# Who subtracts the first 192 columns of a weight slab

## The chip, the cores and the metric

The kernel runs on one core of a Trainium2 chip. The metric is the device time in microseconds (us) of one execution. The engines are TensorE (PE, its weight loads PEld), VectorE (DVE), ScalarE (ACT), GpSimd (POOL) and SyncE (SP), which here only starts DMAs. Each runs its own list of instructions in order, and they meet at semaphores.

## The reference

A sequence of 256 tokens of width 1024 goes through two stacks of two layers each. All products have fp32 weights. Cut to what matters:

```
for i in range(2):                                  # first stack
    proj = rmsnorm(x) @ w_in[i]                     # q, k, v, conv, ssm input, gates
    x = x + (gates * (attention, short conv, s5 scan)) @ w_mix_o[i]
    gt, up = split(rmsnorm(x) @ w_ffn_in[i])
    x = x + (silu(gt) * up) @ w_ffn_out[i]
x = rmsnorm(x)
for l in range(2):                                  # second stack
    u = rmsnorm(x) @ w_in_2[l]                      # retention, ssd, dt, gates
    x = x + (gates * (retention, ssd)) @ w_o_2[l]
    x = x + (silu(gate) * up) @ w_down_2[l]         # as above, other weights
return rmsnorm(x)
```

## The kernel before

All weights are one stream of 696 slabs of 128 x 1024 fp32 in DRAM, read in order (136 slabs for each layer of the first stack, 212 for each of the second). A slab is eight blocks of 128 x 128. To keep the precision, each slab is split in two fp32r halves: `w_hi` is the slab cast to fp32r, `w_lo` is `w_raw - w_hi`. Activations are split in the same way, and each product is three matmuls (L550 hi*hi, L551 hi*lo, L552 lo*hi; in slabs whose result is wanted by rows, L620 to L622), so an ordinary slab costs PE 24 matmuls of 256 columns.

A slab passes through a ring of four slots (`RING`), and the work on it is ordered by semaphores:

- SP loads slab s into `w_raw[s % 4]` when `w_lo` of slab s-4 is done.
- ACT casts it to `w_hi` (L1011) when it has landed and PE has finished slab s-4, and bumps `hi_done`. In ACT's list this cast stands three slabs ahead (`AHEAD`), between its other work.
- POOL subtracts columns 192 to 1023 (L509, `lo_g`). It has nothing else to do after its start: it goes from slab to slab as fast as `hi_done` comes.
- DVE subtracts columns 0 to 191 (L1316, `lo_v`), by a call `split(at, i + AHEAD)` that is written into its list of work at the head of each slab's other work. Whatever stands before it in DVE's list comes first.
- PE starts a slab when both `lo_v` and `lo_g` have come (L539) and the PSUM bank is free.

The order of PE, ACT and DVE is written out by hand in `tasks1`, `tasks2` and `ffn`. Three places are spoken of below.

**The first half of the feed-forward part** (44 slabs, in each of the four layers; a loop over pairs of slabs, gate and up, 88 pairs in all). For each pair b, DVE scales the gate bank (L1366, `f_act`), ACT applies SiLU to it (L1051), DVE multiplies it by the up bank (L1370), scales the product (L1372), casts it to `f_hi` (L1376) and subtracts for `f_lo` (L1378). DVE has a `split` behind L1366 and one behind L1372. ACT casts one slab before the SiLU of a pair and one behind it:

```
split(now, si + 2 * b + 1 + AHEAD)
act.wait_ge(v_gate, now.ffn + (b + 1))
nc.scalar.activation(f_act[:, b, :], f_act[:, b, :], ACT.Silu).then_inc(out[(ti + 2 * b) % 4], 1)
split(now, si + 2 * b + 2 + AHEAD)
```

The SiLU frees the gate's bank, in which PE puts the gate of pair b + 2.

**The value slabs of the second stack** (16 slabs in 8 pairs in each layer, L620 to L622). DVE has nothing to evacuate here; it computes the softplus for `dt`, a chain of some twenty dependent operations on 128 x 64 elements (L1745 to L1770), and stands its splits behind it.

**The gate slabs and the ssd output slabs of the second stack**, where DVE's list holds the roots (L1794 to L1798), the turned `xdt` (L1806), `cbm` (L1814) and the normed `s_hi`, `s_lo` (L1844 to L1849), and PE waits for them.

Of the kernel before, what the change touches and what calls it, by code (L numbers as in the profile page):

```python
# [20 lines left out]
ALU = mybir.AluOpType  # L21
# [13 lines left out]
RING = 4  # L35
AHEAD = 3
LO_V = 192
FF = 22
# [171 lines left out]
def hybrid_kernel(nc, weights, x_t, p1_d, p2_d, c1_d, c2_d, decay_d, out_t):  # L210
    with ExitStack() as ctx:
# [137 lines left out]
        hi_done = sem("hi_done")  # L349
        lo_v = sem("lo_v")  # L350
        lo_g = sem("lo_g")
# [129 lines left out]
        def _(sp):  # L481
# [6 lines left out]
            with sp.Fori(1, TOTAL // RING + 1) as it:  # L488
                for slot in range(RING):

                    sp.wait_ge(lo_v, it * RING + (slot + 1 - RING))
                    sp.wait_ge(lo_g, it * RING + (slot + 1 - RING))
                    load(it * RING + slot, slot)
# [9 lines left out]
        @block.gpsimd  # L503
        def _(pool):
            nc.gpsimd.memset(zpad[:, 0:8], 0.0).then_inc(pad_ok, 1)
            with pool.Fori(0, TOTAL // RING) as it:
                for slot in range(RING):
                    pool.wait_ge(hi_done, it * RING + (slot + 1))
                    nc.gpsimd.tensor_tensor(w_lo[:, slot, LO_V:], w_raw[:, slot, LO_V:],  # L509
                                            w_hi[:, slot, LO_V:].bitcast(F32), ALU.subtract).then_inc(lo_g, 1)  # L510
            for slot in range(AHEAD):
                pool.wait_ge(hi_done, TOTAL + slot + 1)
                nc.gpsimd.tensor_tensor(w_lo[:, slot, LO_V:], w_raw[:, slot, LO_V:],
                                        w_hi[:, slot, LO_V:].bitcast(F32), ALU.subtract).then_inc(lo_g, 1)


        @block.tensor
        def _(pe):
# [13 lines left out]
            def weights_of(at, i):  # L532

                pe.wait_ge(lo_v, at.slab + (i + 1))
                pe.wait_ge(lo_g, at.slab + (i + 1))
# [759 lines left out]
        def _(dve):  # L1295
# [15 lines left out]

            def split(at, i):

                slot = i % RING
                dve.wait_ge(hi_done, at.slab + (i + 1))
                tt(w_lo[:, slot, 0:LO_V], w_raw[:, slot, 0:LO_V], w_hi[:, slot, 0:LO_V].bitcast(F32), SUB).then_inc(lo_v, 1)  # L1316

            def gained(at, second, b):
# [34 lines left out]
            def ffn(at, second):  # L1353
                si, ti, so, to = ffn_layout(second)
                gained(at, second, KD - 1)
                split(at, si + AHEAD)
                root_of(at, 1)
                with dve.Fori(0, FF // 2) as it:
                    now = Later(at, it, 4, 4, 2)
                    for b in range(2):  # L1360
# [5 lines left out]
                        tt(f_act[:, b, :], acc[(t - 1) % 4][:, 0:T], rinv[:, :], MUL).then_inc(v_gate, 1)  # L1366
                        split(now, gate_slab + 1 + AHEAD)
                        wait_used(dve, now, gate_slab + 1)
# [3 lines left out]
                        tt(f_prod[:, b, :], f_prod[:, b, :], rinv[:, :], MUL).then_inc(v_prod, 1)  # L1372
                        split(now, gate_slab + 2 + AHEAD)
                        dve.wait_ge(v_prod, now.ffn + (b + 1))
# [4 lines left out]
                for n in range(KD):  # L1379
                    for m in range(3):  # L1380
                        if n or m:
                            split(at, so + 3 * n + m + AHEAD)
                    wait_used(dve, at, so + 3 * n + 2)
# [211 lines left out]
            def first_slab(at, own, i):  # L1595
                split(at, i + AHEAD)
                bank = acc[i % 4]
# [63 lines left out]
            dve.wait_ge(consts, 32)  # L1661
            start = Layer(False, 0)
            for slot in range(AHEAD):
                split(start, slot)
            dve.wait_ge(pad_ok, 1)
# [465 lines left out]
```

## Time and profile before

| | us |
|---|---|
| median of 3 runs | 2668.67 (2667.32 to 2669.65) |
| span of the profiled execution | 2667.1 |
| PE busy | 2381.9 (89%) |
| DVE busy | 1792.1 (67%) |
| POOL busy | 1486.3 (56%) |
| ACT busy | 1240.4 (47%) |
| DMA read | 373.5 MB, 140 GB/s over the span |

The profiled execution's time is its span, 2667.1 us, 1.6 us below the median. A busy share is an average over stages with different limits, so it doesn't say which engine sets the time; for that one asks in each stage which wait ends last. A row of the timeline gives the start, the duration, and in brackets how long the engine stood idle before it and for whom. "Busy" contains the time that an instruction spends blocked after its start.

### The profile page before, as it was taken

The page shows a single profiled execution, that of the slowest core. Times are in us where ns is not written, and L with a number is a line of the kernel's source. Part 1 is how long each engine was busy: PE and PEld are TensorE (multiplying, and loading weights), DVE is VectorE, ACT ScalarE, POOL GpSimd, SP SyncE. Part 2 cuts the span into 40 slices and gives each one's busy share as a digit, 9 for nine tenths or more (in the row PEclk, how much of TensorE's full clock was granted, in tenths as well). Part 3 has the DMA queues.
Part 4 walks back from the last instruction along what each step waited for, and adds up shares of the span by engine and source line. Part 5 has one row for each costly group of instructions (what it writes and reads, how often), then busy time and mean ns, then how long its engine had stood idle before and what let it go on. Part 6 is the DMA issues. An engine that isn't in the chain of part 4 may idle for free.

```text
span 2667.1 us, 53618 instructions
## 1 busy us (share of the span) xinstructions
PE 2381.9 (89%) x18844; PEld 2281.2 (86%) x18844; DVE 1792.1 (67%) x2602; ACT 1240.4 (47%) x1744; POOL 1486.3 (56%) x704
## 2 busy tenths in 40 slices
PE   5798699987787899988989998999889989979998
PEld 5788699887787899888989888999889889879988
DVE  5876769738976499284784467696465773485992
ACT  4243355542243555443543662654435536645554
POOL 4344466664444466755546455667565555456666
PEclk9899899988888899989999999999899999999999
DMA  4233344543233354544434334445544344334444
GB/s 162 91 108 103 103 150 164 175 160 103 88 111 111 111 167 168 193 143 144 141 113 165 127 111 158 155 164 178 167 147 160 122 140 146 119 127 166 165 161 171
DMA packets 104265, 377.19 MB, mean 141 GB/s; under 512 B 11408, under 2 KB 13712, under 8 KB 103824
## 3 DMA queue, kind: packets, MB, share of 16 engines
q1 hardware_dynamic: 101888, 368.10, 40.5%
q10 hardware_dynamic: 2192, 6.52, 0.7%
q8 instruction: 129, 2.11, 0.3%
q14 instruction: 56, 0.46, 0.1%
HBM read 373.52 MB, written 1.05 MB: 140 GB/s over the span
## 4 chain that ended last, share of the span: by engine, by line
PE 57%; DVE 26%; issue 11%; ACT 5%; DVEq 1%; DMA 1%; ACTq 0%
PE acc L550 15%; PE acc L551 14%; PE acc L552 14%; DVE f_hi L1376 6%; ACT w_hi L1011 2%; PE mid L673 2%; DVE zs L1509 1%; PE mid L524 1%; DVE w_lo L1316 1%; DVE f_act L1366 1%; PE acc L620 1%; PE acc L621 1%; PE acc L622 1%; DVE r_hi L1868 1%; PE mid L901 1%
## 5 line engine op out<-in xcount | busy, mean ns | idle before, releaser
L509 POOL TENSOR_TENSOR w_lo<-w_raw,w_hi 128x832 fp32r<-128x832 f32 x696 | 1479.6, 2132 | 1168.1 <-ACT w_hi L1011 1166.5
L1011 ACT CAST w_hi<-w_raw 128x1024 fp32r<-128x1024 f32 x699 | 726.6, 1047 | 401.1 <-PE acc L552 384.0
L550 PE MATMUL acc<-h_hi,w_hi 128*128 128x256 f32 x2240 | 665.8, 297 | 55.9 <-DVE w_lo L1316 45.9
L1316 DVE TENSOR_TENSOR w_lo<-w_raw,w_hi 128x192 fp32r<-128x192 f32 x699 | 394.4, 569 | 453.7 <-ACT w_hi L1011 434.0
L551 PE MATMUL acc<-h_lo,w_hi 128*128 128x256 f32 x2240 | 647.1, 289 | 0.0
L552 PE MATMUL acc<-h_hi,w_lo 128*128 128x256 f32 x2240 | 645.7, 288 | 0.0
L550 PEld LDWEIGHTS acc<-h_hi,w_hi 128*128 128x128 f32 x2240 | 444.1, 198 | 66.6 <-DVE w_lo L1316 48.3
L551 PEld LDWEIGHTS acc<-h_lo,w_hi 128*128 128x128 f32 x2240 | 444.2, 198 | 0.8
L552 PEld LDWEIGHTS acc<-h_hi,w_lo 128*128 128x128 f32 x2240 | 443.0, 198 | 0.0
L550 PE MATMUL acc<-g_hi,w_hi 128*128 128x256 f32 x1376 | 397.1, 289 | 10.1 <-ACT f_act L1051 0.5
L552 PE MATMUL acc<-g_hi,w_lo 128*128 128x256 f32 x1376 | 386.4, 281 | 0.0
L551 PE MATMUL acc<-g_lo,w_hi 128*128 128x256 f32 x1376 | 386.3, 281 | 0.0
L550 PEld LDWEIGHTS acc<-g_hi,w_hi 128*128 128x128 f32 x1376 | 259.4, 189 | 33.4 <-issue 23.2
L551 PEld LDWEIGHTS acc<-g_lo,w_hi 128*128 128x128 f32 x1376 | 259.6, 189 | 0.0
L552 PEld LDWEIGHTS acc<-g_hi,w_lo 128*128 128x128 f32 x1376 | 259.4, 188 | 0.0
L550 PE MATMUL acc<-f_hi,w_hi 128*128 128x256 f32 x704 | 205.8, 292 | 15.3 <-DVE f_lo L1378 13.7
L552 PE MATMUL acc<-f_hi,w_lo 128*128 128x256 f32 x704 | 200.0, 284 | 0.0
L551 PE MATMUL acc<-f_lo,w_hi 128*128 128x256 f32 x704 | 199.9, 284 | 0.0
L1378 DVE TENSOR_TENSOR f_lo<-f_prod,f_hi 128x256 f32 x88 | 183.6, 2086 | 10.8
L1376 DVE CAST f_hi<-f_prod 128x256 f32 x88 | 181.0, 2057 | 0.0
L550 PEld LDWEIGHTS acc<-f_hi,w_hi 128*128 128x128 f32 x704 | 135.5, 192 | 18.3 <-DVE f_lo L1378 14.5
L1051 ACT ACTIVATE f_act<-f_act 128x256 f32<-128x256 f32 x88 | 36.9, 420 | 229.1 <-DVE f_act L1366 229.0
(347 smaller groups left out, 4317.1 us busy)
## 6 DMA issues: line engine op xcount, KB each, us to landing
w_raw<-weights_d SPq DMA_DIRECT2D x700, 512.0 KB, 3.3
p<-p_d ACTq DMA_DIRECT2D x2, 1080.0 KB, 5.4
rdec<-decay_d ACTq DMA_DIRECT2D x2, 768.0 KB, 5.7
x<-x_d ACTq DMA_DIRECT2D x1, 1024.0 KB, 11.3
out_d<-work SPq DMA_DIRECT2D x4, 256.0 KB, 2.2
c<-c_d ACTq DMA_DIRECT2D x1, 712.0 KB, 12.4
p<-p_d ACTq DMA_DIRECT2D x2, 244.0 KB, 2.8
c<-c_d ACTq DMA_DIRECT2D x1, 448.0 KB, 4.0
```

The lines of the kernel that those rows point to most:

```text
L509: nc.gpsimd.tensor_tensor(w_lo[:, slot, LO_V:], w_raw[:, slot, LO_V:], w_hi[:, slot, LO_V:].bitcast(F32), ALU.subtract).then_inc(lo_g, 1)
L524: part = mm(mid[0][:, 0:T], con1("ones_d"), work[:, b, :], start=b == 0, stop=b == KD - 1)
L550: mm(dst, wh, hi[:, k, :], start=first and j == 0, stop=False)
L551: mm(dst, wh, lo[:, k, :], start=False, stop=False)
L552: done = mm(dst, wl, hi[:, k, :], start=False, stop=last and j == len(ks) - 1)
L620: mm(dst, hh, wh, start=k == 0, stop=False)
L673: last = mm(dst, b, u[rows, blk, c * CH:(c + 1) * CH], start=True, stop=True, tile_position=(PC * q, 0))
L1011: nc.scalar.copy(w_hi[:, slot, :], w_raw[:, slot, :]).then_inc(hi_done, 1)
L1051: nc.scalar.activation(f_act[:, b, :], f_act[:, b, :], ACT.Silu).then_inc(out[(ti + 2 * b) % 4], 1)
L1316: tt(w_lo[:, slot, 0:LO_V], w_raw[:, slot, 0:LO_V], w_hi[:, slot, 0:LO_V].bitcast(F32), SUB).then_inc(lo_v, 1)
L1376: copy(f_hi[:, k, :], f_prod[:, b:b + 1, :]).then_inc(ff_hi, 1)
L1378: tt(f_lo[:, k, :], f_prod[:, b:b + 1, :], f_hi[:, k, :].bitcast(F32), SUB).then_inc(ff_lo, 1)
```

## The change

The constant `LO_V` and DVE's `split` go. POOL subtracts all 1024 columns of each slab. The semaphore `lo_v` goes, and with it SP's wait and PE's wait for it. Nothing else is moved.

```diff
-LO_V = 192
...
-                    sp.wait_ge(lo_v, it * RING + (slot + 1 - RING))
                     sp.wait_ge(lo_g, it * RING + (slot + 1 - RING))
                     load(it * RING + slot, slot)
...
-                    nc.gpsimd.tensor_tensor(w_lo[:, slot, LO_V:], w_raw[:, slot, LO_V:],
-                                            w_hi[:, slot, LO_V:].bitcast(F32), ALU.subtract).then_inc(lo_g, 1)
+                    nc.gpsimd.tensor_tensor(w_lo[:, slot, :], w_raw[:, slot, :],
+                                            w_hi[:, slot, :].bitcast(F32), ALU.subtract).then_inc(lo_g, 1)
...
-                pe.wait_ge(lo_v, at.slab + (i + 1))
                 pe.wait_ge(lo_g, at.slab + (i + 1))
...
-            def split(at, i):
-
-                slot = i % RING
-                dve.wait_ge(hi_done, at.slab + (i + 1))
-                tt(w_lo[:, slot, 0:LO_V], w_raw[:, slot, 0:LO_V], w_hi[:, slot, 0:LO_V].bitcast(F32), SUB).then_inc(lo_v, 1)
...
                         tt(f_act[:, b, :], acc[(t - 1) % 4][:, 0:T], rinv[:, :], MUL).then_inc(v_gate, 1)
-                        split(now, gate_slab + 1 + AHEAD)
...
                         tt(f_prod[:, b, :], f_prod[:, b, :], rinv[:, :], MUL).then_inc(v_prod, 1)
-                        split(now, gate_slab + 2 + AHEAD)
                         dve.wait_ge(v_prod, now.ffn + (b + 1))
...
             def second_slab(at, own, i):
-                split(at, i + AHEAD)
```

The other calls of `split` in DVE's list (in `first_slab`, in the second half of the feed-forward part and three at the start) go in the same way.

DVE's list in the first half of the feed-forward part, one pair, before; the names in brackets are the semaphores waited for:

```order
L1366 TENSOR_TENSOR f_act<-acc,rinv 128x256 [waits out3,used]
L1316 TENSOR_TENSOR w_lo<-w_raw,w_hi 128x192 [waits hi_done]
L455 REGISTER_ALU
L1370 TENSOR_TENSOR f_prod<-f_act,acc 128x256 [waits out2,used]
L1372 TENSOR_TENSOR f_prod<-f_prod,rinv 128x256 [waits out3]
L1316 TENSOR_TENSOR w_lo<-w_raw,w_hi 128x192 [waits hi_done]
L1374 REGISTER_ALU
L1376 ISA [waits v_prod]
L1376 COPY f_hi<-f_prod 128x256
L1378 REGISTER_ALU [waits ff_hi]
L1378 TENSOR_TENSOR f_lo<-f_prod,f_hi 128x256
```

The same pair now (the lines have moved up by 11 to 13):

```order
L1355 TENSOR_TENSOR f_act<-acc,rinv 128x256 [waits out3,used]
L453 REGISTER_ALU
L1358 TENSOR_TENSOR f_prod<-f_act,acc 128x256 [waits out2,used]
L1360 TENSOR_TENSOR f_prod<-f_prod,rinv 128x256 [waits out3]
L1361 REGISTER_ALU
L1363 ISA [waits v_prod]
L1363 COPY f_hi<-f_prod 128x256
L1365 REGISTER_ALU [waits ff_hi]
L1365 TENSOR_TENSOR f_lo<-f_prod,f_hi 128x256
```

The two subtractions are gone and the cast to `f_hi` stands directly behind the second product.

DVE's list at the value slabs, the end of the `dt` chain, before:

```order
L1768 SCALAR_TENSOR_TENSOR dts<-dts 128x64 [waits dve_step2]
L1769 REGISTER_ALU
L1770 SCALAR_TENSOR_TENSOR dts<-dts 128x64 [waits dve_step2]
L1315 REGISTER_ALU
L1316 TENSOR_TENSOR w_lo<-w_raw,w_hi 128x192 [waits hi_done]
L1315 REGISTER_ALU
L1316 TENSOR_TENSOR w_lo<-w_raw,w_hi 128x192 [waits hi_done]
```

And now:

```order
L1748 SCALAR_TENSOR_TENSOR dts<-dts 128x64 [waits dve_step2]
L1749 REGISTER_ALU
L1750 SCALAR_TENSOR_TENSOR dts<-dts 128x64 [waits dve_step2]
L1712 ISA
L1715 SCALAR_TENSOR_TENSOR cv<-acc,p_130,cv 128x255 [waits a_cv]
```

Nothing that PE needs for its value slabs stands behind the chain any more; the next thing in the list is the convolution of the slabs that follow.

## Rows read from the trace of the kernel before

**Rows 1.** The page: the chain that ended last, shares of the span by engine.
```profile
PE 57%; DVE 26%; issue 11%; ACT 5%; DVEq 1%; DMA 1%; ACTq 0%
```

**Rows 2.** Waits of PE on VectorE's share: us in total, times, longest us.
```profile
PE acc L550 <- DVE w_lo L1316: 57.4, 14, 8.0
PE acc L620 <- DVE w_lo L1316: 13.4, 2, 6.7
```

**Rows 3.** Groups and single lines: durations in ns, minimum/median/maximum or mean.
```profile
L1316 DVE TENSOR_TENSOR w_lo<-w_raw,w_hi 128x192 fp32r<-128x192 f32 x699 | 394.4, 569 | 453.7 <-ACT w_hi L1011 434.0
...
L509 POOL TENSOR_TENSOR w_lo<-w_raw,w_hi x696: 1926/2146/4034, 5.5 to 2646.4; 128x832 fp32r<-128x832 f32 x174
L505 POOL MEMSET zpad<- x1: 105/105/105, 0.7 to 0.7; 128x8 f32 x1
L1376 DVE CAST f_hi<-f_prod x88: 2021/2048/2093, 373.6 to 2592.2; 128x256 f32 x88
L1378 DVE TENSOR_TENSOR f_lo<-f_prod,f_hi x88: 1980/2004/2200, 375.7 to 2594.4; 128x256 f32 x88
```

**Rows 4.** Timeline of VectorE, feed-forward, second layer: start us, duration us, what.
```profile
956.55 0.41 DVE L1366 TENSOR_TENSOR f_act<-acc,rinv 128x256 f32<-128x256 f32 x1
...
957.45 0.42 DVE L1370 TENSOR_TENSOR f_prod<-f_act,acc 128x256 f32<-128x256 f32 x1 [0.22 <-ACT f_act L1051]
957.90 0.42 DVE L1372 TENSOR_TENSOR f_prod<-f_prod,rinv 128x256 f32<-128x256 f32 x1
958.39 0.36 DVE L1316 TENSOR_TENSOR w_lo<-w_raw,w_hi 128x192 fp32r<-128x192 f32 x1
958.71 2.03 DVE L1376 CAST f_hi<-f_prod 128x256 f32 x1
960.86 2.00 DVE L1378 TENSOR_TENSOR f_lo<-f_prod,f_hi 128x256 f32 x1
962.78 0.41 DVE L1366 TENSOR_TENSOR f_act<-acc,rinv 128x256 f32<-128x256 f32 x1
...
967.10 2.20 DVE L1378 TENSOR_TENSOR f_lo<-f_prod,f_hi 128x256 f32 x1
969.23 0.41 DVE L1366 TENSOR_TENSOR f_act<-acc,rinv 128x256 f32<-128x256 f32 x1
```

**Rows 5.** Timelines of GpSimd and ScalarE in the same stretch.
```profile
958.43 4.15 POOL L509 TENSOR_TENSOR w_lo<-w_raw,w_hi 128x832 fp32r<-128x832 f32 x2 [2.08 <-ACT w_hi L1011]
964.67 2.17 POOL L509 TENSOR_TENSOR w_lo<-w_raw,w_hi 128x832 fp32r<-128x832 f32 x1 [2.09 <-ACT w_hi L1011]
967.03 1.99 POOL L509 TENSOR_TENSOR w_lo<-w_raw,w_hi 128x832 fp32r<-128x832 f32 x1 [0.20 <-ACT w_hi L1011]
...
957.00 0.42 ACT L1051 ACTIVATE f_act<-f_act 128x256 f32<-128x256 f32 x1 [1.41 <-DVE f_act L1366]
957.32 1.99 ACT L1011 CAST w_hi<-w_raw 128x1024 fp32r<-128x1024 f32 x2
```

**Rows 6.** Timeline of PE there: first matmul of a gate slab, of an up slab.
```profile
957.47 0.39 PE L550 MATMUL acc<-g_hi,w_hi 128*128 128x256 f32 x1
...
960.69 0.36 PE L550 MATMUL acc<-g_hi,w_hi 128*128 128x256 f32 x1
```

**Rows 7.** Value slabs: stretches with busy us (x matmuls first) and PEclk; PE's wait.
```profile
1237.10:1242.70 5.60, 5.57 (x26) 5.58 (x27) 0.51 (x2) 0.00 (x0) 0.00 (x0) 0.51 0.75 257
1997.10:2002.70 5.60, 5.54 (x34) 5.55 (x35) 0.54 (x3) 0.00 (x0) 0.00 (x0) 0.71 0.75 257
1245.30:1251.10 5.80, 5.80 (x50) 5.77 (x49) 1.56 (x2) 2.54 (x4) 4.14 (x2) 1.00 0.14 34
...
1237.13 0.58 PE L620 MATMUL acc<-w_hi,h_hi 128*128 128x256 f32 x1 [6.72 <-DVE w_lo L1316]
```

**Rows 8.** Gate and ssd slabs: the same columns (us, PE, PEld, DVE, ACT, POOL).
```profile
1354.70:1402.40 47.70, 34.68 (x267) 33.16 (x265) 46.43 (x74) 17.21 (x26) 25.79 (x12) 0.90 0.33 111
1588.20:1621.20 33.00, 19.47 (x130) 18.45 (x128) 32.10 (x40) 9.70 (x13) 15.70 (x7) 0.90 0.18 64
```

More of the change, by code:

```diff
@@ L349, in hybrid_kernel @@
         hi_done = sem("hi_done")
-        lo_v = sem("lo_v")
         lo_g = sem("lo_g")
@@ L508, in _ @@
                     pool.wait_ge(hi_done, it * RING + (slot + 1))
-                    nc.gpsimd.tensor_tensor(w_lo[:, slot, LO_V:], w_raw[:, slot, LO_V:],
-                                            w_hi[:, slot, LO_V:].bitcast(F32), ALU.subtract).then_inc(lo_g, 1)
+                    nc.gpsimd.tensor_tensor(w_lo[:, slot, :], w_raw[:, slot, :],
+                                            w_hi[:, slot, :].bitcast(F32), ALU.subtract).then_inc(lo_g, 1)
             for slot in range(AHEAD):
                 pool.wait_ge(hi_done, TOTAL + slot + 1)
-                nc.gpsimd.tensor_tensor(w_lo[:, slot, LO_V:], w_raw[:, slot, LO_V:],
-                                        w_hi[:, slot, LO_V:].bitcast(F32), ALU.subtract).then_inc(lo_g, 1)
+                nc.gpsimd.tensor_tensor(w_lo[:, slot, :], w_raw[:, slot, :],
+                                        w_hi[:, slot, :].bitcast(F32), ALU.subtract).then_inc(lo_g, 1)
         @block.tensor
@@ L1355, in ffn @@
                 gained(at, second, KD - 1)
-                split(at, si + AHEAD)
                 root_of(at, 1)
@@ L1379, in ffn @@
                 for n in range(KD):
-                    for m in range(3):
-                        if n or m:
-                            split(at, so + 3 * n + m + AHEAD)
                     wait_used(dve, at, so + 3 * n + 2)
@@ L1661, in _ @@
             dve.wait_ge(consts, 32)
-            start = Layer(False, 0)
-            for slot in range(AHEAD):
-                split(start, slot)
             dve.wait_ge(pad_ok, 1)
@@ L1851, in second_slab @@
             def second_slab(at, own, i):
-                split(at, i + AHEAD)
                 bank = acc[i % 4]
```

## Prediction, made before the changed kernel ran

> **What bounds the kernel now.** I read the chain that ended last, then PE's waits, then each stage's timeline. The chain runs 57% over PE and 26% over VectorE, and not at all over GpSimd by name [rows 1]. That is where care is needed: a VectorE instruction that is blocked by GpSimd counts as VectorE's.
>
> The chip shows the block plainly in the first half of the feed-forward part. VectorE's cast to f_hi and its subtraction for f_lo take 2.0 to 2.2 us in all 88 pairs [rows 3], while a product of the same 256 columns takes 0.42 [rows 4]. The cast starts at 958.71, 0.28 us after a GpSimd subtraction that started at 958.43, and ends at 960.74; the two GpSimd instructions there take 4.15 together, so the first ends near 960.5. The f_lo subtraction starts at 960.86 and ends at 962.86, behind the second one (958.43 + 4.15 = 962.58) [rows 4, 5]. On the other side, VectorE's share of w_lo at 958.39 starts 0.04 before GpSimd and takes 0.36, undisturbed [rows 4, 5]. At 967.10 an f_lo subtraction that starts 0.07 after GpSimd is blocked for 2.20. The rule that I read from this: of two such instructions the one that starts first keeps the other out until it ends; products with an operand in PSUM (f_act, the first f_prod) are free. The Trainium skill, SBUF — State Buffer, section "SBUF: two separate sides", calls it an exclusive lock on a port pair that GpSimd shares with VectorE, taken by VectorE's two-input operations and its two-port modes; by that rule, the trace agrees.
>
> So a pair of slabs there is a closed loop: f_act starts, SiLU on ScalarE, ScalarE's casts of w_hi, two GpSimd subtractions, the end of f_lo, next f_act. It takes 962.78 - 956.55 = 6.23 us in one parity and 969.23 - 962.78 = 6.45 in the other, 6.34 on average. PE is a passenger: it starts a gate slab at 957.47, 0.05 after SiLU has freed the bank, and an up slab at 960.69, just after GpSimd's w_lo [rows 5, 6]. PE needs 48 matmuls for the pair, at the full clock 50 of them in 5.8 us [rows 7], so 5.6 us: it has 0.7 us to spare in each.
>
> Elsewhere PE waits directly for VectorE's share of w_lo, 57.4 + 13.4 = 71 us in 16 places [rows 2]. There the subtraction itself is short; it stands behind other VectorE work.
>
> **The GpSimd instruction.** Undisturbed, 832 columns take 1.93 us, the minimum [rows 3]; the median 2.15 has about 0.2 us of waiting for VectorE's share, which starts just before. 8 columns of a memset take 0.105 [rows 3]. So (1.93 - 0.10) / 832 = 2.2 ns per column, and 192 more cost 0.42 us: 2.35. In proportion to the median it would be 2.15 x 1024 / 832 = 2.64, 0.49 more; against that median an instruction that no longer waits would be only 0.2 longer. I take 0.42 where GpSimd starts freely now, 0.2 where it waits for VectorE's share, and keep 0.2 to 0.49 as bounds. The Trainium skill, GPSIMD Engine Reference, section 3.1, gives 4497 ns for a tensor_tensor of 2048 fp32 columns, so by estimate 2.25 us for 1024, against 2293 ns on VectorE, and its rule for elementwise work is to use VectorE. By that price the sum below would be 0.1 us smaller in each GpSimd instruction.
>
> **Feed-forward, first half: +48 us.** The two shares of w_lo leave VectorE's list (0.34 and 0.36 a pair). The first lies under the wait for SiLU: f_prod starts 0.03 after SiLU ends in any case, so nothing comes back. The second lets the cast to f_hi move up. How far decides the case. From the end of f_hi (960.74) to the start of f_lo, which waits for it, is 0.12 us [rows 4], and the cast waits in the same way for the product that ends at 957.90 + 0.42 = 958.32, with one register instruction of 0.07 in place of 0.04. So it would start at 958.44 to 958.48. GpSimd starts at 958.43, set by ScalarE alone. The cast comes 0.01 to 0.05 too late. In the other parity the product ends 0.1 later against GpSimd, so the cast is clearly too late. I take it that the cast stays blocked; then both GpSimd instructions stay in the loop, and each is longer:
> - first parity: the first one loses its 0.2 wait and gains 0.42 (+0.2), the second gains 0.42: 6.23 + 0.62 = 6.85;
> - second parity: the first one (2.17) becomes 2.35 and ends when ScalarE's second cast arrives anyway (967.03), so +0; the second gains 0.42 to 0.5: 6.45 + 0.46 = 6.91.
>
> On average +0.54, times 88 pairs = +48 us. PE does not limit this (5.6 of 6.9) and the second half of the part begins only when the last f_lo is there, so the whole loop counts. With the bounds of the instruction it is +35 (0.4 a pair) to +60 (0.68).
>
> **Value slabs: -15 us.** PE waits at 1237.13 for 6.7 us on VectorE's share, which stands behind the dt chain, in both layers [rows 2, 7]. Nothing else is missing there: PE's banks are emptied by ScalarE. The wait goes, 13.4 us. So does what follows it: after the wait PE's granted clock is 0.51 of full over 5.6 us (its 1.2 GHz level for nearly all of it), with 26 matmuls where the full clock gives 48, and in the second layer 0.71 with 34 [rows 7]; 22 and 14 matmuls at 0.117 are 2.6 and 1.6 us. Together 17.6. What is late next is GpSimd: a pair of slabs frees two slots at once, ScalarE and GpSimd then work on two slabs in a row (4.14 us in 5.8 [rows 7]), and 2 x 0.2 more makes them later than PE. Some four pairs in each layer pay 0.4: +3. The sum is -15, and -8 to -18 as bounds.
>
> **Gate and ssd output slabs: -5 us.** VectorE is busy 46.4 of 47.7 us and 32.1 of 33.0 [rows 8]; PE's waits for w_lo there are followed by waits for xdt, cbm and s_lo behind the same list. So removing a wait moves it to the next place, and only VectorE's own saving counts. The first stretch has 10 shares of w_lo and 12 GpSimd instructions, the second 4 and 7. If all is exclusive: 10 x 0.36 less, 12 x 0.42 more, that is +1.4; and 4 x 0.36 less, 7 x 0.42 more, +1.5. If a share had been the one that was blocked (mean 0.57, so 0.2 of blocking each [rows 3]) and much of GpSimd's time lies under PSUM work, it is -5 and -2. I take -2.5 for the two together, twice: -5, with +6 to -14 as bounds.
>
> **First stack outside the feed-forward part: 0.** By the same account: VectorE's lists there (turning factors, scans) hold the long two-operand operations, PE's waits for w_lo move to the rotary and scan results behind them. A slab costs the shared resource 1.93 + 0.34 = 2.27 now and 2.35 then. Over 68 slabs in each of two layers the difference is 0.08 x 136 = +11 where it is all on the path, and VectorE's freedom not to wait for w_hi in order (434 us idle [rows 3]) works against it. I take 0, -10 to +11.
>
> SP loads when GpSimd has finished instead of when both have, up to 0.4 us later; with four slots nothing waits for that. The second half of the feed-forward part has nearly no VectorE work and more than 2.35 us of PE per slab: 0.
>
> **Sum.** 48 - 15 - 5 = +28 on the span of 2667.1: 2695. The median stands 1.6 above the span, so 2697.
>
> **Rivals.**
> *The cast wins.* If the cast to f_hi starts before GpSimd in the first parity (it misses by 0.01 to 0.05 us; a start 0.04 before was enough [rows 4, 5]), it takes 0.3 instead of 2.0, and f_lo is blocked by the first GpSimd instruction alone. The next f_act starts at about 1.88 + 0.3 + 2.35 + 0.2 = 4.7. The second instruction then reaches into the next pair and blocks its second product until 7.1, so that pair loses: the cast is behind GpSimd, f_lo too, and it ends at 7.1 + 2 x 2.4 + 0.6 = 12.4. Two pairs in 12.4 us against 12.68 now: -0.14 a pair, -12 in all. The time is 2667 - 12 - 15 - 5 = 2635, 2637 on the measure. This is the case on the other side, and it decides at a few tens of ns at one place. For it: the margin. Against: all 88 f_lo, which start a like distance behind GpSimd, are blocked.
> *VectorE relieved everywhere.* PE's 71 us of waits for w_lo come back whole and the loop stays at 6.34: 2667 - 71 = 2596, 2598. For it: the list of waits. Against: the busy VectorE behind those waits [rows 8] and GpSimd in the loop.
> *Even.* GpSimd grows by 0.2 only, or the loop mixes won and lost casts: +15 to +20 in the feed-forward part against -20: 2662 to 2674.
> *GpSimd is the bound.* At 2.64 it would take nearly all of the 2.8 us of a slab at PE's pace, and each VectorE operation with two SBUF operands would wait for a boundary: the loop +60, other stages +25: 2735.
>
> **How the numbers follow.** Forecast (the loop lengthens) 0.66, the cast wins 0.16, even 0.09, relieved 0.04, GpSimd the bound 0.05. The likeliest alone spans 2680 to 2712. The range reaches to the second case: 2636 to 2713, which leaves out about 2 in 10. A measurement here can't tell less than 0.2%, 5.3 us, from no change. Slower by more than that: 0.66 + 0.05 = 0.71 and a little of even, 0.72; faster: 0.16 + 0.04 = 0.20; within: 0.08.
>
> **What would show it.** Right: GpSimd's minimum at 2.35; in the feed-forward part f_act every 6.8 to 6.9 us; 88 casts of 2.4 us; PE's wait at the value slabs gone and the clock at 1.00 behind it; waits on xdt, cbm, s_lo and the rotary results as long as the w_lo waits before them. Wrong: casts of 0.3 us in every second pair, or a period under 6.34; or PE reaching the value slabs' end late because of GpSimd. The forecast falls first with the order of two starts that are 0.05 us apart.

## The result, and the profile after

The changed kernel takes 2716.45 us (median of 4 runs, 2715.84 to 2717.57), the kernel before, run beside it, 2668.49: a ratio of 1.0184, 95% interval 1.0170 to 1.0199. It is 48 us slower. Forecast were +28 and 2697, with a range up to 2713: the direction was right, the size was not.

The page of the changed kernel, the parts that answer to [rows 1] and the table above:

```profile
span 2714.6 us, 51537 instructions
...
PE 2382.5 (88%) x18844; PEld 2277.5 (84%) x18844; DVE 1603.1 (59%) x1903; ACT 1238.5 (46%) x1744; POOL 1733.3 (64%) x704
...
issue 44%; POOL 33%; PE 15%; DVE 6%; ACT 1%; POOLq 1%; DVEq 0%; ACTq 0%
```

VectorE is busy 189 us less, GpSimd 247 more, and the chain that ended last now runs 33% over GpSimd, where it ran over GpSimd by name not at all [rows 1]. VectorE's shares alone were 394 us [rows 3], so all its other instructions together stand some 205 us longer than before: that is blocked time, counted as busy.

PE's waits of the changed kernel that answer to [rows 2] (us in total, times, longest). VectorE's `w_lo` is gone from the list; GpSimd's is short each time; but the waits for the rotary products, the scan states, `s_lo` and `xdt` are longer. In the kernel before these four were 12.6, 25.9, 6.0 and 4.8 us. PE also waits for ScalarE's `f_act`, which frees its banks in the feed-forward loop: 31.9 us in 72 places, 2.1 before.

```profile
PE mid L682 <- DVE xst L1523: 41.4, 4, 11.7
PE acc L546 <- ACT f_act L1047: 31.9, 72, 0.6
PE mid L692 <- DVE qk L1462: 31.5, 2, 15.9
...
PE acc L546 <- DVE s_lo L1829: 26.2, 16, 7.9
...
PE acc L546 <- POOL w_lo L506: 20.3, 76, 0.3
...
PE mid L872 <- DVE xdt L1786: 15.8, 5, 5.9
```

Where the time went. The spans are cut at the end of the last matmul of each stage's last slab, so they add up to the whole span. Us, sums over both layers of a stack (the feed-forward part over all four); the row of before is absolute, the others are differences from it. The rows below the forecast belong to the experiments of the next section. Each row comes from one profiled execution, and that of narrow_880 took 7 us more than its kernel's median.

| | first stack | FFN, first half | FFN, second half | value slabs | gate slabs | ssd output | rest | span |
|---|---|---|---|---|---|---|---|---|
| before | 714.7 | 545.7 | 283.4 | 117.4 | 148.5 | 238.6 | 618.9 | 2667.1 |
| after | +3.5 | +43.9 | +8.6 | -14.7 | +3.4 | +4.0 | -1.2 | +47.5 |
| forecast | 0 | +48 | 0 | -15 | -5 with ssd output | (see left) | 0 | +28 |
| alone_v | +0.6 | -0.4 | -0.2 | -14.6 | +1.7 | -0.6 | -1.5 | -14.9 |
| share_ffn | +2.3 | -0.4 | -1.7 | -14.6 | +7.0 | +4.3 | -0.9 | -3.8 |
| narrow (832) | -25.5 | -41.0 | -23.9 | -17.8 | -7.7 | -2.1 | -0.7 | -118.8 |
| narrow_880 | -19.3 | -38.9 | -11.5 | -17.1 | -4.3 | -0.4 | 0.0 | -91.5 |
| narrow_928 | -14.2 | +16.5 | +2.1 | -16.3 | +2.8 | +2.8 | -1.8 | -8.2 |
| hi_first | +2.6 | -12.9 | -2.8 | -14.7 | +6.8 | +4.8 | -1.1 | -17.3 |
| share_late | +0.1 | -25.5 | -11.0 | +1.0 | +0.8 | 0.0 | -0.8 | -35.4 |
| after_psum_hi | +6.1 | -41.0 | -23.9 | -14.7 | +5.8 | +2.9 | -1.7 | -66.5 |
| alone_v_psum_late | +0.2 | -43.3 | -24.9 | -14.6 | +1.8 | -0.8 | -1.9 | -83.5 |
| share_384 | -12.6 | -41.0 | -23.9 | -3.3 | -5.7 | -7.0 | -0.6 | -94.1 |
| alone_v_384 | -19.8 | -41.0 | -23.9 | -14.6 | -6.0 | -7.8 | -1.5 | -114.7 |
| alone_v_512 | -31.5 | -39.6 | -22.9 | -14.6 | -6.1 | -10.1 | -1.4 | -126.3 |

Four kernels do the same work in the gate slabs (after, share_ffn, hi_first and after_psum_hi) and differ by up to 3.6 us there, so differences of that size in one cell are not read.

The feed-forward loop of the changed kernel, the stretch that answers to [rows 4, 5]: VectorE, then GpSimd.

```profile
961.86 0.41 DVE L1355 TENSOR_TENSOR f_act<-acc,rinv 128x256 f32<-128x256 f32 x1
...
963.21 0.42 DVE L1360 TENSOR_TENSOR f_prod<-f_prod,rinv 128x256 f32<-128x256 f32 x1
963.79 2.49 DVE L1363 CAST f_hi<-f_prod 128x256 f32 x1 [0.15 <-DVE f_prod L1360]
966.40 2.41 DVE L1365 TENSOR_TENSOR f_lo<-f_prod,f_hi 128x256 f32 x1
968.73 0.41 DVE L1355 TENSOR_TENSOR f_act<-acc,rinv 128x256 f32<-128x256 f32 x1
...
963.74 4.78 POOL L506 TENSOR_TENSOR w_lo<-w_raw,w_hi 128x1024 fp32r<-128x1024 f32 x2 [2.09 <-ACT w_hi L1007]
```

The cast starts at 963.79, 0.05 behind GpSimd, and is blocked; f_lo is blocked by the second GpSimd instruction. The period is 968.73 - 961.86 = 6.87 here and 6.92 in the pair before it (forecast 6.85 and 6.91).

The stretches of the changed kernel that answer to [rows 7]: behind the start of the value slabs, and the third and fourth slab of the second half of a feed-forward part (us; then PE, PEld, DVE, ACT, POOL busy with counts; PEclk).

```profile
1242.30:1247.90 5.60, 5.60 (x49) 5.60 (x47) 0.00 (x0) 2.78 (x5) 4.09 (x2) 1.00 0.17 57
1093.40:1105.40 12.00, 7.45 (x43) 7.24 (x42) 6.03 (x5) 4.25 (x5) 9.58 (x4) 0.72 0.54 176
```

The first shows the gain: full clock, 49 matmuls where [rows 7] has 26. The second shows a loss that the prediction did not have: 43 matmuls in 12 us, at a granted clock of 0.72.

### The profile page after: what moved, and what is told of

Read it like the earlier page. It is cut to its first block, busy times and chain, and to the rows that moved or that the text cites. A ratio compares the mean times of both kernels' runs of the same rounds, so it can differ in the third digit from the quotient of the medians.

```text
span 2714.6 us, 51537 instructions
## 1 busy us (share of the span) xinstructions
PE 2382.5 (88%) x18844; PEld 2277.5 (84%) x18844; DVE 1603.1 (59%) x1903; ACT 1238.5 (46%) x1744; POOL 1733.3 (64%) x704
## 3 DMA queue, kind: packets, MB, share of 16 engines
q8 instruction: 130, 2.13, 0.3%
## 4 chain that ended last, share of the span: by engine, by line
issue 44%; POOL 33%; PE 15%; DVE 6%; ACT 1%; POOLq 1%; DVEq 0%; ACTq 0%
POOL w_lo L506 33%; PE acc L546 4%; PE acc L547 4%; PE acc L548 4%; DVE f_hi L1363 2%; PE mid L897 0%; DVE pr L1843 0%; POOLq L503 0%; DVE f_prod L1360 0%; DVE f_prod L1358 0%; PE mid L913 0%; ACT f_act L1047 0%; POOLq L505 0%; DVE pr L1845 0%; DVE f_act L1355 0%
## 5 line engine op out<-in xcount | busy, mean ns | idle before, releaser
L506 POOL TENSOR_TENSOR w_lo<-w_raw,w_hi 128x1024 fp32r<-128x1024 f32 x696 | 1725.9, 2489 | 969.5 <-ACT w_hi L1007 965.6
L546 PE MATMUL acc<-h_hi,w_hi 128*128 128x256 f32 x2240 | 661.5, 295 | 11.5 <-DVE h_lo L1630 11.5
L546 PEld LDWEIGHTS acc<-h_hi,w_hi 128*128 128x128 f32 x2240 | 441.1, 197 | 20.2 <-DVE h_lo L1630 12.4
L546 PE MATMUL acc<-f_hi,w_hi 128*128 128x256 f32 x704 | 207.2, 294 | 21.4 <-DVE f_lo L1365 18.2
L1363 DVE CAST f_hi<-f_prod 128x256 f32 x88 | 215.8, 2452 | 13.9 <-DVE f_prod L1360 10.9
L1365 DVE TENSOR_TENSOR f_lo<-f_prod,f_hi 128x256 f32 x88 | 213.4, 2425 | 10.8
L1368 DVE TENSOR_TENSOR x<-x,acc 128x256 f32<-128x256 f32 x32 | 13.5, 421 | 227.3 <-PE acc L548 227.3
```

The source lines that it names most:

```text
L506: nc.gpsimd.tensor_tensor(w_lo[:, slot, :], w_raw[:, slot, :], w_hi[:, slot, :].bitcast(F32), ALU.subtract).then_inc(lo_g, 1)
L546: mm(dst, wh, hi[:, k, :], start=first and j == 0, stop=False)
L1363: copy(f_hi[:, k, :], f_prod[:, b:b + 1, :]).then_inc(ff_hi, 1)
L1365: tt(f_lo[:, k, :], f_prod[:, b:b + 1, :], f_hi[:, k, :].bitcast(F32), SUB).then_inc(ff_lo, 1)
L1368: tt(x[:, n, :], x[:, n, :], acc[(to + n) % 4][:, 0:T], ADD).then_inc(out[(to + n) % 4], 1)
```

## Experiments

**Which stages the loss is in.** Two kernels do one part of the change each. In the first GpSimd is alone only at the value slabs, in the second everywhere but in the feed-forward parts. A list of slab ranges decides: there GpSimd starts at column 0, and VectorE counts `lo_v` up once for a whole range that it doesn't touch. The list is that of alone_v; in share_ffn it is `[(4, 68)], [(4, 144)]`:

```diff
+ALONE = [], [(16, 32)]
...
+            for a, b, alone in stretches():
+                v = 0 if alone else LO_V
...
                 slot = i % RING
+                alone = run_of(at.second, i)
+                if alone:
+                    if i == alone[0]:
+                        dve.wait_ge(lo_v, at.slab + i)
+                        dve.sem_inc(lo_v, alone[1] - alone[0])
+                    return
```

> The kernel before, with one part of the change: GpSimd subtracts whole slabs alone only at the 16 value slabs of each layer of the second stack (16 to 31); VectorE keeps its 192 columns everywhere else. Theory (the prediction's): PE's waits of 6.7 us and the half clock behind them go, +3 for the longer GpSimd instruction, nothing is given back later: 15 us less, 2653 (2650 to 2658). Rival: the wait goes to the next place that hangs on the same VectorE list (the convolution slabs behind the dt chain), and nothing is gained: 2666 to 2669.

Measured: 2652.8 us (10 runs), ratio 0.9957, interval 0.9942 to 0.9972; by the stages -14.6 at the value slabs and -14.9 over the whole span. The gain at the value slabs is whole and nothing behind it gives it back.

> VectorE keeps its 192 columns only in the feed-forward parts (and the 4 slabs behind each); GpSimd is alone in all other slabs, as in the changed kernel. Theory: the loss of the changed kernel is the feed-forward loop's (+52 by the stages) and the rest (value slabs -15, gate and ssd output +7, first stack +4) stands as it is: 2716 - 52 = 2664 (2660 to 2668), pairs of 6.34 us again. Rival: the loss is made by GpSimd's longer instruction wherever it stands, also before the feed-forward part, whose slabs start late: then 2680 or more and pairs above 6.5.

Measured: 2663.99 (10 runs), ratio 1.0000, 0.9986 to 1.0014. The feed-forward loop is back to its 545.3 us. With VectorE's columns back in the feed-forward parts the span is 2714.6 - 2663.2 = 51 us shorter: the loss of the changed kernel is made there. The two kernels together also show the rest: outside the feed-forward part and the value slabs, GpSimd alone costs 2663.2 - 2652.2 = 11 us, and there the forecast had -5.

**Length of the instruction, or emptied list?** The changed kernel with the short instruction; it leaves out the correction of 192 columns, whose `w_lo` stays zero:

```diff
+            nc.gpsimd.memset(w_lo[:, :, 0:192].bitcast(F32), 0.0)
...
-                    nc.gpsimd.tensor_tensor(w_lo[:, slot, :], w_raw[:, slot, :],
-                                            w_hi[:, slot, :].bitcast(F32), ALU.subtract).then_inc(lo_g, 1)
+                    nc.gpsimd.tensor_tensor(w_lo[:, slot, 192:], w_raw[:, slot, 192:],
+                                            w_hi[:, slot, 192:].bitcast(F32), ALU.subtract).then_inc(lo_g, 1)
```

> The changed kernel, but GpSimd subtracts 832 of the 1024 columns, as long as before; the other 192 are set to zero once and left out of the computation. It has VectorE's emptied list without the longer GpSimd instruction. Theory of the lock (two blocked VectorE instructions in a closed loop; elsewhere the two engines' times add up): feed-forward pairs 6.03 in one parity, 6.4 in the other, -9 in all; value slabs -18; gate and ssd output -10; first stack between -5 and -46 (136 shares of 0.34): 2605 to 2635. Rival, waits only move behind the same list: nothing outside the value slabs and the pairs: 2640. Rival, the length of the instruction is not what the changed kernel lost by: 2700 or more.

Measured: 2548.73 (4 runs), ratio 0.956, 0.9532 to 0.9587. That is 56 us below the lowest expectation, and all of the surprise lies in the feed-forward part: -65 where -9 was expected. The timeline of narrow, one pair: VectorE, GpSimd, ScalarE.

```profile
963.99 2.01 DVE L1364 CAST f_hi<-f_prod 128x256 f32 x1 [0.16 <-DVE f_prod L1361]
966.12 0.42 DVE L1366 TENSOR_TENSOR f_lo<-f_prod,f_hi 128x256 f32 x1
966.77 0.42 DVE L1356 TENSOR_TENSOR f_act<-acc,rinv 128x256 f32<-128x256 f32 x1 [0.23 <-PE acc L549]
...
963.87 1.98 POOL L507 TENSOR_TENSOR w_lo<-w_raw,w_hi 128x832 fp32r<-128x832 f32 x1 [2.09 <-ACT w_hi L1008]
966.23 2.17 POOL L507 TENSOR_TENSOR w_lo<-w_raw,w_hi 128x832 fp32r<-128x832 f32 x1 [0.38 <-ACT w_hi L1008]
...
962.75 1.04 ACT L1008 CAST w_hi<-w_raw 128x1024 fp32r<-128x1024 f32 x1
963.81 1.28 ACT L1008 ACT_TABLE_LOAD   x1
965.10 1.05 ACT L1008 CAST w_hi<-w_raw 128x1024 fp32r<-128x1024 f32 x1
```

In every second pair ScalarE loads a table between its two casts of `w_hi` (1.28 us). GpSimd's second instruction, which waits for the second cast, then doesn't start before 966.23, 4.24 after f_act (at 961.99), while the first one ended at 965.85. f_lo is ready at 966.12, in this gap, and takes 0.42 instead of 2.0. The pair takes 4.8 us, the other 6.3, and PE now sets the pace: VectorE waits for it (the last bracket). In the kernel before, the same f_lo starts at 967.10 and GpSimd's second instruction at 967.03 [rows 4, 5]: 0.07 too late, since the first one had waited for VectorE's share and took 2.17. In narrow 40 of the 88 f_lo go through such a gap, in the kernel before none. So there is a window, and a new theory: the loop's time doesn't follow the length of the instruction but jumps where f_lo misses it. Two widths on either side of the computed edge test this.

> The changed kernel with 880 of 1024 columns subtracted by GpSimd (the other 144 set to zero once and left out). Which law joins the narrow run (832: 2549) and the changed kernel (1024: 2716)? Theory of the window: by the slope 880 columns take 2.03 us, the first instruction of a pair ends 3.91 us after f_act, f_lo is ready at 4.19, before GpSimd's second one at 4.24 (ScalarE's table load sets that): f_lo goes first in every second pair, the loop stays at PE's pace, 126 us for the first half; the rest of the kernel grows by a quarter of its difference: 2560 to 2570. Rival, the loop grows with the length of the instruction from 832 columns on: a quarter of the way, 2590 (2585 to 2600).

Measured: 2570.8 (4 runs), ratio 0.9634, 0.9615 to 0.9653, 0.8 us above the range of the theory of the window and 14 us below that of the linear one; first half 506.8 / 4 = 126.7 us per layer.

> The same with 928 columns. Theory of the window: 2.14 us, the first instruction ends 4.02 after f_act, f_lo is ready at 4.30, 0.06 behind the second GpSimd instruction, and is blocked in every pair: pairs jump to 6.45 to 6.65, the first half to 139 to 143 us, the second half to 70.8, 2645 to 2665. Rival, linear: half of the way, 2632 (2625 to 2640), first half at 137 or less.

Measured: 2657.71 (5 runs), ratio 0.997, 0.9951 to 0.9989; first half 562.2 / 4 = 140.6 per layer. 48 columns more, 0.1 us of an instruction, and the first half loses 13.9 us per layer; the 48 below that cost 0.5. The two kernels at the edge, first 880 columns, then 928 (VectorE, GpSimd):

```profile
968.19 0.43 DVE L1366 TENSOR_TENSOR f_lo<-f_prod,f_hi 128x256 f32 x1
...
968.20 2.38 POOL L507 TENSOR_TENSOR w_lo<-w_raw,w_hi 128x880 fp32r<-128x880 f32 x1 [0.28 <-ACT w_hi L1008]
```

```profile
958.71 2.37 DVE L1366 TENSOR_TENSOR f_lo<-f_prod,f_hi 128x256 f32 x1
...
958.61 2.19 POOL L507 TENSOR_TENSOR w_lo<-w_raw,w_hi 128x928 fp32r<-128x928 f32 x1 [0.17 <-ACT w_hi L1008]
```

0.01 us ahead of GpSimd f_lo takes 0.43; 0.10 behind it takes 2.37, and with 928 columns f_lo is blocked in all 88 pairs. The kernel with 880 columns stands on the edge itself. In 40 of its pairs f_lo starts within 0.013 us of GpSimd: 35 of these are free, at starts shown from 0.013 ahead of GpSimd to 0.005 behind it, and 5 take 2.36, at 0.010 to 0.013 behind. The window decides, not the slope.

The zeros are not what made these kernels fast: after_psum_hi and share_384 below compute every column and reach the same 126.2 us per layer as narrow in the first half.

**Does a cast that wins do what the prediction's first rival said?**

```diff
                         tt(f_prod[:, b, :], f_act[:, b, :], acc[t % 4][:, 0:T], MUL).then_inc(out[t % 4], 1)
                         wait_out(dve, now, t)
+                        k = bass.ds(it * 2 + b, 1)
+                        tt(f_hi[:, k, :], f_prod[:, b:b + 1, :], rinv[:, :].unsqueeze(1), MUL).then_inc(ff_hi, 1)
                         tt(f_prod[:, b, :], f_prod[:, b, :], rinv[:, :], MUL).then_inc(v_prod, 1)
                         dve.wait_ge(v_prod, now.ffn + (b + 1))
-                        k = bass.ds(it * 2 + b, 1)
-                        copy(f_hi[:, k, :], f_prod[:, b:b + 1, :]).then_inc(ff_hi, 1)
```

> The changed kernel, but f_hi is written by a product of its own, f_prod times rinv rounded to F32R, ahead of the second product, instead of a cast of that product's result. So it starts some 0.5 us earlier, about 0.5 us ahead of GpSimd, and the second product follows at once, about level with GpSimd's start. Theory of the lock: f_hi is out of GpSimd's way, only f_lo is blocked once, the loop is below PE's own time, and a pair takes PE's 5.6 to 6.0 us instead of 6.89: -80 to -110, 2606 to 2636. If the second product loses to GpSimd it is blocked in place of the cast and the pair stays near 6.8: 2705 to 2716. Rival, GpSimd's w_lo comes late for PE whatever VectorE does: no change, 2716.

Measured: 2649.99 (5 runs), ratio 0.994, 0.992 to 0.9961. This lies between the two theories, and for a reason that the prediction had named under its first rival. VectorE's timeline of hi_first:

```profile
954.86 0.41 DVE L1355 TENSOR_TENSOR f_act<-acc,rinv 128x256 f32<-128x256 f32 x1
...
956.67 0.42 DVE L1362 TENSOR_TENSOR f_prod<-f_prod,rinv 128x256 f32<-128x256 f32 x1
...
959.55 0.41 DVE L1355 TENSOR_TENSOR f_act<-acc,rinv 128x256 f32<-128x256 f32 x1
...
961.09 1.09 DVE L1361 TENSOR_TENSOR f_hi<-f_prod,rinv 128x256 f32 x1 [0.15 <-DVE f_prod L1358]
962.10 2.62 DVE L1362 TENSOR_TENSOR f_prod<-f_prod,rinv 128x256 f32<-128x256 f32 x1
964.85 2.41 DVE L1365 TENSOR_TENSOR f_lo<-f_prod,f_hi 128x256 f32 x1
967.18 0.41 DVE L1355 TENSOR_TENSOR f_act<-acc,rinv 128x256 f32<-128x256 f32 x1
```

The winning pair takes 4.69; GpSimd's second instruction then reaches into the next one, which is blocked three times and takes 7.63. Two pairs: 12.32 us (the prediction's rival had 12.4). In the second pair the product starts at 962.10, 0.24 behind the GpSimd instruction that the trace starts at 961.86, and is blocked.

**Products that GpSimd doesn't block.** The factor rinv goes in before the bank is read, so that the two products behind it have an operand in PSUM:

```diff
                         tt(f_act[:, b, :], acc[(t - 1) % 4][:, 0:T], rinv[:, :], MUL).then_inc(v_gate, 1)
+                        wait_out(dve, now, t - 1)
+                        tt(f_act[:, b, :], f_act[:, b, :], rinv[:, :], MUL).then_inc(v_prod, 1)
                         wait_used(dve, now, gate_slab + 1)
-                        wait_out(dve, now, t - 1)
+                        dve.wait_ge(v_prod, now.ffn + (b + 1))
+                        k = bass.ds(it * 2 + b, 1)
+                        tt(f_hi[:, k, :], f_act[:, b:b + 1, :], acc[t % 4][:, 0:T].unsqueeze(1), MUL).then_inc(ff_hi, 1)
                         tt(f_prod[:, b, :], f_act[:, b, :], acc[t % 4][:, 0:T], MUL).then_inc(out[t % 4], 1)
                         wait_out(dve, now, t)
-                        tt(f_prod[:, b, :], f_prod[:, b, :], rinv[:, :], MUL).then_inc(v_prod, 1)
-                        dve.wait_ge(v_prod, now.ffn + (b + 1))
-                        k = bass.ds(it * 2 + b, 1)
-                        copy(f_hi[:, k, :], f_prod[:, b:b + 1, :]).then_inc(ff_hi, 1)
```

> The changed kernel, GpSimd alone with 1024 columns, but the feed-forward products written otherwise: f_act times rinv first, then f_hi and f_prod each as that times the bank in PSUM. The first product starts 0.9 us after f_act, a microsecond ahead of GpSimd, the two with a PSUM operand are not blocked by it, and only f_lo is left in GpSimd's way. Theory of the lock: the loop falls below PE's own time, pairs 5.6 to 5.8 us: 29.6 less in each of four layers, 2598 (2592 to 2612). Rival: as in the run with f_hi ahead, GpSimd's instructions run into the next pair in every second one and block the first product there, pairs 6.1: 2640 to 2655. Rival: products with a PSUM operand are held up too: 2690 or more.

Measured: 2601.89 (4 runs), ratio 0.9755, 0.9739 to 0.9771, with GpSimd still alone on 1024 columns. VectorE's groups of it (busy us and mean ns behind the bar):

```profile
L1365 DVE TENSOR_TENSOR f_lo<-f_prod,f_hi 128x256 f32 x88 | 153.0, 1739 | 10.8
L1357 DVE TENSOR_TENSOR f_act<-f_act,rinv 128x256 f32<-128x256 f32 x88 | 134.6, 1529 | 82.1 <-ACT f_act L1047 82.1
...
L1361 DVE TENSOR_TENSOR f_hi<-f_act,acc 128x256 f32 x88 | 37.1, 422 | 14.0 <-DVE f_act L1357 11.0
```

f_hi is no longer blocked once in 88. But the expectation, that only f_lo would be left in GpSimd's way, was wrong: the new product on L1357 has both operands in SBUF and takes 1.53 us on average where an undisturbed one takes 0.42. Two instructions of a pair are blocked here too. What fell is how long: the two stand 1.53 + 1.74 = 3.3 us in each pair, where the cast and f_lo of the changed kernel stand 2.45 + 2.43 = 4.9 (their means on its page). So GpSimd's 2.4 us instructions are no trouble for PE in this part by themselves (the first half takes 126.2 us a layer, as in narrow); the +52 came over the time that VectorE's chain stands blocked in the loop, and goes when that chain is written otherwise.

**VectorE's share moved, widened, and the parts together.** share_late does the second share of a pair one pair later, behind f_act:

```diff
                         tt(f_act[:, b, :], acc[(t - 1) % 4][:, 0:T], rinv[:, :], MUL).then_inc(v_gate, 1)
+                        split(now, gate_slab + AHEAD)
                         split(now, gate_slab + 1 + AHEAD)
...
-                        split(now, gate_slab + 2 + AHEAD)
```

> The kernel before, with VectorE's second share of w_lo in each feed-forward pair moved: it is done one pair later, right after f_act, beside the first share, so nothing of VectorE's holds up the first GpSimd instruction of a pair. GpSimd still has 832 columns. Theory, from the run with the narrow instruction: in every second pair ScalarE loads a table of functions between its two casts of w_hi, so GpSimd's second instruction can't start before 4.24 us after f_act starts; f_lo is ready at 4.13 if the first one was not held up, and goes first. In the kernel before it is 0.07 too late. Then two pairs take 11.1 to 11.4 us instead of 12.7 and the second half of the part starts without a wait: 40 to 65 us less, 2603 to 2627. Rival: the moved shares are themselves blocked after f_act and delay the products, pairs stay at 6.2 to 6.4: 2655 to 2675.

Measured: 2629.69 (4 runs), ratio 0.9858, 0.9841 to 0.9874. The feed-forward part brings -36.5, where 40 to 65 less were expected. f_lo is free in both kinds of pairs now (0.43, 76 of the 88), but the moved shares are blocked behind f_act in every second pair, which was the rival's mechanism. Both happen, and the loop ends at 6.86 + 4.80 us for two pairs (f_act at 955.25, 962.11 and 966.91).

share_384 changes one number of the kernel before, LO_V = 384:

> The kernel before, with the change's number turned the other way: VectorE subtracts 384 columns and GpSimd 640. By the slope of the two widths GpSimd takes 1.5 us, VectorE some 0.6. Theory: what counts is how long GpSimd holds VectorE off: the first instruction of a pair ends 3.9 us after f_act although it waits for the longer share, f_lo goes ahead of the second one in every second pair, the loop falls to PE's 5.6 (-64 with the second half); elsewhere a slab costs the two engines together 0.14 less (-20 over 164 slabs in the stages that VectorE bounds): 2583 (2570 to 2600). Rival: VectorE's longer share makes PE's waits for w_lo behind VectorE's list grow, in value slabs, output slabs and rotary slabs: +0.26 a share, and the loop keeps 6.2: 2650 or more.

Measured: 2574.52 (4 runs), ratio 0.9648, 0.9632 to 0.9664. VectorE does more of the work and the kernel is 92 us faster. The feed-forward part goes to PE's pace, and gate and ssd output slabs gain 12.7.

> The best of the parts together: GpSimd alone at the value slabs only, 832 columns elsewhere; the feed-forward products written with PSUM operands as in after_psum_hi, and VectorE's second share of a pair moved behind the next f_act. Theory: value slabs -15 and a feed-forward part at PE's pace (-64) add up against the kernel before: 2589 (2583 to 2600). Rival: the two shares behind f_act are blocked by GpSimd's last instruction of the pair before and make the loop the bound again: 2610 to 2650.

Measured: 2584.23 (4 runs), ratio 0.9688, 0.9672 to 0.9704. The two gains, at the value slabs and in the feed-forward part, add.

> VectorE subtracts 384 columns and GpSimd 640, but at the value slabs GpSimd is alone. Theory: the two gains add where they don't overlap: 2574.5 for 384 columns alone, of which 2.5 and 0.8 in the value slabs, against 7.8 and 6.9 for GpSimd alone there: 2563 (2559 to 2568). Rival: GpSimd's 2.35 us per slab at the value slabs, behind slabs of 1.5, makes no difference to be seen or loses: 2572 or more.

Measured: 2557.3 (4 runs), ratio 0.9594, 0.9576 to 0.9613. The gains add; it is 2 us below the theory's range, from 7 us less in the first stack than share_384, which no term of the theory had: both subtract the same columns there, so the cause is open.

> The same with half of each slab for either engine. By the slopes 512 columns cost GpSimd 1.23 us and VectorE 0.69, together 1.92 instead of 2.06 with 384. Theory, the two engines' times add up in the stages that VectorE bounds: 0.14 a slab, some 10 us less than with 384: 2553 (2547 to 2560). Rival: VectorE's longer share now makes PE wait for w_lo behind VectorE's list, and ends level with 384 or above: 2563 or more.

Measured: 2537.89 (4 runs), ratio 0.9508, 0.9483 to 0.9533: 129 us less than the kernel before, 179 less than the changed kernel, the best version here. It is 9 below the theory's 2547 to 2560; the first stack alone gained 11.7 over alone_v_384, where GpSimd's instruction went from 1.53 to 1.26 us (the minima). Widths beyond 512 weren't tried.

## Why the prediction fell short, point by point

**GpSimd's instruction: right.** Its minimum is 2.33 us (forecast 2.35), 0.40 more. The minima of the other widths, 1.26 at 512, 1.53 at 640, 1.93 at 832, 2.03 at 880, 2.13 at 928, give 2.1 ns a column against the 2.2 that came from one memset. The Trainium skill, GPSIMD Engine Reference, section 3.1, led to an estimate of 2.25, which is 0.08 short; the 2293 ns for VectorE that the prediction sets beside it is that section's figure for 2048 columns, not for 1024. Its advice to give such work to VectorE is borne out up to half of a slab: 192, 384 and 512 columns on VectorE are each better than none.

**The block itself: right, on thinner rows than it says.** The prediction reads from [rows 4] that products with an operand in PSUM are free. In those rows no GpSimd instruction is under way when such a product starts, so they can't show it. after_psum_hi does: all 88 f_prod start with a GpSimd subtraction under way and take 0.41 to 0.42 us.

**Feed-forward: the loop right, its end mis-sized.** Period, blocked cast and the 0.05 us of the two starts came as forecast; +43.9 in the first half. The second half was put at 0 and cost +8.6. The loop's last f_lo is also what PE waits for in the third slab of the second half (18.2 us in 4 places, up to 4.6 each; 13.7 and 3.5 before), so part of the loop's loss is paid there. Behind the wait PE's clock is lower for longer: from 1099.8 to 1105.4 it does 26 matmuls in 5.6 us at a granted 0.52, where the kernel before did 26 in the 4.2 us from 1070.9 at 0.62. Over the whole 12 us shown above the clock is 0.72. The same two slabs in the kernel before (the same columns), 10 us at 0.84:

```profile
1065.10:1075.10 10.00, 6.60 (x44) 6.40 (x43) 9.83 (x9) 3.80 (x4) 8.21 (x4) 0.84 0.47 156
```

narrow, which has no such wait, goes through them at 1.00 and is 23.9 faster in the second halves. The step that failed here is "The second half of the feed-forward part has nearly no VectorE work and more than 2.35 us of PE per slab: 0": it looked at the slabs and not at the seam between the halves. Together the two halves cost 52.5 against 48, so this is 4.5 us of the miss.

**Value slabs: right.** -14.7 against -15, with full clock and 49 matmuls where 26 were.

**Gate and ssd output slabs: the wrong value taken.** This is the step that failed most. The prediction worked out "all exclusive", +1.4 and +1.5 a layer, so +5.8, and then took -2.5 a layer for the two together. Measured: +3.4 and +4.0, +7.4 (the other three kernels with GpSimd alone there: +8.7 to +11.6). The runs take it apart: narrow has the emptied list without the length and gives -7.7 and -2.1, close to all of the shares in the stretches of [rows 8] removed (20 x 0.36 = 7.2, 8 x 0.36 = 2.9). From narrow to the changed kernel it is +11.1 and +6.1, close to all of the lengthening there (24 x 0.42 = 10.1, 14 x 0.42 = 5.9). So GpSimd's longer time counted about in full, and no large part of it lay under PSUM work for free. The whole stages have more slabs than those stretches (16 and 32 a layer), so the agreement is one of size, not a proof.

The argument for -2.5 was that shares had been blocked, mean 0.57, and would take that blocking away with them. The gain of narrow, 9.8 us for the 28 shares of those stretches, is 0.35 a share and not 0.57: the time of the work went, the blocking stayed. The gate chain, four VectorE instructions in a row, shows it: the kernel before, then narrow, then the changed kernel.

```profile
L1868 DVE CAST r_hi<-pr 128x256 fp32r<-128x256 f32 x32 | 34.4, 1074 | 1.1
...
L1870 DVE TENSOR_TENSOR r_lo<-pr,r_hi 128x256 fp32r<-128x256 f32 x32 | 23.9, 746 | 1.1
...
L1866 DVE TENSOR_TENSOR pr<-pr,rr 128x256 f32<-128x256 f32 x32 | 18.7, 585 | 1.1
...
L1864 DVE TENSOR_TENSOR pr<-sg,yr 128x256 f32<-128x256 f32 x32 | 13.3, 417 | 6.9 <-ACT sg L1016 6.8
```

```profile
L1844 DVE TENSOR_TENSOR pr<-sg,yr 128x256 f32<-128x256 f32 x32 | 29.4, 920 | 10.0 <-ACT sg L1013 9.8
L1850 DVE TENSOR_TENSOR r_lo<-pr,r_hi 128x256 fp32r<-128x256 f32 x32 | 27.1, 847 | 1.1
...
L1846 DVE TENSOR_TENSOR pr<-pr,rr 128x256 f32<-128x256 f32 x32 | 20.2, 632 | 1.1
...
L1848 DVE CAST r_hi<-pr 128x256 fp32r<-128x256 f32 x32 | 16.1, 504 | 1.1
```

```profile
L1849 DVE TENSOR_TENSOR r_lo<-pr,r_hi 128x256 fp32r<-128x256 f32 x32 | 38.4, 1200 | 1.1
...
L1845 DVE TENSOR_TENSOR pr<-pr,rr 128x256 f32<-128x256 f32 x32 | 34.6, 1080 | 1.1
...
L1843 DVE TENSOR_TENSOR pr<-sg,yr 128x256 f32<-128x256 f32 x32 | 27.8, 869 | 8.7 <-ACT sg L1012 8.3
...
L1847 DVE CAST r_hi<-pr 128x256 fp32r<-128x256 f32 x32 | 13.7, 429 | 1.1
```

Their means sum to 2.82 us before, 2.90 in narrow and 3.58 in the changed kernel. With GpSimd's length unchanged and the shares gone (narrow) the chain is blocked as much as before, only in other instructions; the longer GpSimd instruction then adds 0.68 us to it, more than its own 0.40, since more than one of the four can be blocked. The worst place is the start of the ssd output slabs. There GpSimd does four subtractions in a row (10.78 us from 1618.34), and beside them VectorE takes 5.01 us for two products, 2.45 for the cast s_hi and 2.71 for s_lo, where the next group of the same four takes 0.88, 0.43 and 0.69; PE waits 7.9 us for it, once in each layer, where it waited 4.7 for `w_lo` in the kernel before.

**First stack outside the feed-forward part: within its bounds.** Forecast 0, measured +3.5. narrow gives -25.5 of the 46 that all shares would be (136 x 0.34), the length +29.0 of 57 (136 x 0.42): about half of either is on the path. As forecast, the waits only moved: the slabs 4 to 7 of a layer are 10 us faster and the 12 behind them 10 slower, where PE waits 15.9 us instead of 6.3 for the rotary products.

**The sum.** 47.5 - 28 = 19.5 us: gate and ssd output 12.4, feed-forward 4.5, first stack 3.5, value slabs 0.3, rest -1.2. The misses in the gate and ssd output slabs and in the first stack have the sign that follows from one rule that the prediction had and then softened: where VectorE's list bounds a stage, GpSimd's whole length counts. The feed-forward one is the wait at the seam. The mechanism of the forecast and its direction held, and every term but the second half's 0 and the gate and ssd slabs' +6 stayed within its own bounds; the top of the range, 2713, was set only 16 us above the sum of middle values.

**The rivals.** "The cast wins" was not what happened, though its mechanism was right: hi_first made it happen and gave 12.32 us for two pairs, against 12.4 (the terms written out there add up to 12.5). "VectorE relieved everywhere" fell: narrow gains more than PE's 71 us of waits, but 65 of its 119 us come in the feed-forward part by the window, and with the change's own longer instruction nothing of it is left outside the value slabs. What no rival had was that GpSimd's second instruction leaves a gap of which VectorE missed the edge by 0.07 us in the kernel before. Its rows were in [rows 4, 5].

## What to carry to other kernels

Where two engines lock each other out, the cost of a longer instruction is not its own length but what stands behind it: count, for each loop, how many of the other engine's instructions it can block and for how long, and look at the starts that are less than 0.1 us apart, on either side. A share of work moved off a blocked engine takes its work with it, but here left its blocking to the next instruction. Try the number in the other direction too: here 384 and 512 columns on VectorE gained 3.5% and, with GpSimd alone at the value slabs, 4.9%.

## What the runs showed of the hardware

Who starts first decides, to about the hundredth of a us that the trace can tell: with 880 columns the 35 f_lo shown from 0.013 ahead of GpSimd to 0.005 behind it went undisturbed (0.43 us), and the 5 shown 0.010 to 0.013 behind lost 1.9 us. The Trainium skill, SBUF — State Buffer, section "SBUF: two separate sides", says that the first to start holds the ports for its whole instruction; the trace agrees. VectorE's products with an operand in PSUM were not held up: in after_psum_hi all 88 f_prod started while a GpSimd subtraction was under way and took 0.414 us on average.

ScalarE's load of a function table took 1.28 us and stood between two casts of `w_hi` in every second pair only, so that a loop whose body holds the same pair twice had two kinds of rounds. In narrow the gap for f_lo is there in the pairs with the load between the casts (0.38 us between GpSimd's two instructions) and not in the others, where the two run back to back. No run takes the load away, so that it opened the window is read from the trace alone.
